# Expert down weights loaded with rows 128 apart in a partition, and the hidden rows turned by two full transpositions

## The reference, cut to what matters

```python
D_MODEL = 1024
N_EXPERTS = N_GROUPS * EXPERTS_PER_GROUP      # 32
D_EXPERT = D_MODEL // 2                       # 512
...
    def expert_block(args):
        xblk, e = args
        return (jax.nn.silu(xblk @ w1[e]) * (xblk @ w3[e])) @ w2[e]
```

## Time and profile before

| | |
|---|---|
| median of 3 runs | 1860.23 us (1854.81 to 1861.74) |
| the profiled execution | 1857.37 us |
| its span in the profile | 1855.5 us, mean granted clock 0.978 |
| TensorE matmul busy | 1718.4 us (93%) |
| VectorE, ScalarE busy | 714.4 us (38%), 594.6 us (32%) |
| moved by DMA | 341.91 MB in 79581 packets, mean 184 GB/s |

### The profile page before, as it was taken

How to read it: one execution, slowest core, us unless ns; L and a number is a source line. 1 busy time by engine, 2 the same in 40 slices (tenths; PEclk the granted TensorE clock), 3 DMA queues, 4 the chain that set the end, 5 groups by cost and what they waited for, 6 DMA issues and landing times.

```text
span 1855.5 us, 24991 instructions
## 1 busy us (share of the span) xinstructions
PE 1718.4 (93%) x10533; PEld 1317.4 (71%) x10533; DVE 714.4 (38%) x1529; ACT 594.6 (32%) x1048; POOL 169.3 (9%) x128
## 2 busy tenths in 40 slices
PE   6999999997999888888889999998999899999998
PEld 5878766886665555455558966666788798888886
DVE  4355454453111111211136577555734532222223
ACT  3434454422010000000124456554524432222222
POOL 1000110221111111101101000011101000000221
PEclk9999999998999999999999999998999999999999
DMA  6512100348999999999995331013420222223201
GB/s 249 192 46 84 53 23 23 135 190 327 356 405 411 410 407 409 405 410 406 414 354 189 97 112 66 1 46 113 171 92 12 91 103 91 92 89 138 91 23 46
DMA packets 79581, 341.91 MB, mean 184 GB/s; under 512 B 8007, under 2 KB 15815, under 8 KB 66024
## 3 DMA queue, kind: packets, MB, share of 16 engines
q1 hardware_dynamic: 73192, 329.76, 45.7%
q0 software_dynamic: 5120, 8.40, 1.3%
q10 hardware_dynamic: 1152, 2.10, 0.3%
HBM read 329.75 MB, written 18.87 MB: 188 GB/s over the span
## 4 chain that ended last, share of the span: by engine, by line
PE 70%; DMA 19%; DVE 5%; ACT 4%; issue 2%; POOL 0%; SPq 0%; DVEq 0%; POOLq 0%; ACTq 0%
PE ps L553 66%; DMA arenaf<-in_w 14%; DMA arenaf<-in_mem 3%; DMA hf<-in_w_xkv 2%; PE ps L972 1%; PE ps L2874 1%; DMA hd<-xf 1%; PE ps L807 1%; PE ps L2057 1%; DVE arenaf L2956 1%; DVE splitr L618 0%; ACT splitr L629 0%; DVE arenaf L2974 0%; ACT arenaf L961 0%; ACT arenaf L868 0%
## 5 line engine op out<-in xcount | busy, mean ns | idle before, releaser
L553 PE MATMUL ps<-hr,splitr 128*128 128x512 f32 (+1 forms) x2784 | 576.3, 367 | 6.8 <-POOL hr L904 4.3
L553 PEld LDWEIGHTS ps<-hr,splitr 128*128 128x128 f32 x2784 | 474.7, 192 | 87.9 <-issue 5.0
L553 PE MATMUL ps<-splitr,hr 128*128 128x512 f32 (+1 forms) x1488 | 273.7, 343 | 2.2 <-DVE hr L1069 1.4
L553 PEld LDWEIGHTS ps<-splitr,hr 128*128 128x128 f32 x1488 | 234.2, 190 | 35.7 <-issue 2.0
L618 DVE TENSOR_TENSOR splitr<-ring,splitr 128x2048 fp32r<-128x2048 f32 x61 | 142.8, 2343 | 232.9 <-ACT splitr L629 232.8
L629 ACT CAST splitr<-ring 128x2048 fp32r<-128x2048 f32 x61 | 116.1, 1904 | 152.2 <-PE ps L553 142.7
L2089 DVE SCALAR_TENSOR_TENSOR arenaf<-ps,arenaf 128x256 f32<-128x256 f32 x32 | 15.5, 484 | 271.9 <-PE ps L553 244.9
L2125 ACT COPY junk<-ps 64x512 f32<-64x512 f32 x32 | 18.5, 578 | 285.6 <-PE ps L553 285.6
L553 PE MATMUL ps<-arenaf 128*64 128x128 f32 (+7 forms) x784 | 103.1, 342 | 5.5 <-ACT arenaf L979 3.5
L553 PE MATMUL ps<-arenaf,tq 128*64 128x512 f32 x336 | 84.9, 651 | 19.5 <-DMA arenaf<-in_w 19.5
L618 DVE TENSOR_TENSOR splitr<-arenaf,splitr 128x2048 fp32r<-128x2048 f32 x27 | 62.2, 2304 | 104.8 <-ACT splitr L629 104.8
(11 more groups left out here) (397 smaller groups left out, 1959.8 us busy)
## 6 DMA issues: line engine op xcount, KB each, us to landing
ring<-in_w SPq DMA_DIRECT2D x22, 2048.0 KB
arenaf<-in_w SPq DMA_DIRECT2D x22, 2048.0 KB, 43.4
splitf<-in_w SPq DMA_DIRECT2D x21, 2048.0 KB
hf<-in_w SPq DMA_DIRECT2D x20, 2048.0 KB, 43.9
ring<-in_w_in SPq DMA_DIRECT2D x11, 2048.0 KB
otf<-in_w SPq DMA_DIRECT2D x11, 2048.0 KB
ring<-in_w_gate_up SPq DMA_DIRECT2D x7, 2048.0 KB
arenaf<-in_w_in SPq DMA_DIRECT2D x4, 2048.0 KB, 8.5
```

The lines of the kernel that those rows point to most:

```text
L553: return te.matmul(out, lhsT, rhs, start=start, stop=stop)
```

## The change

The w2 loads take the view that dense weights have: partition p gets the rows p, 128 + p, 256 + p and 384 + p, so a load is 512 pieces of 4 KB and no longer 128 pieces of 16 KB. Its bytes and its destination are the same in size. The hidden row is now turned in two blocks of 128 contiguous columns, each one a transposition of all 128 partitions. `pe_down` picks the 64-column groups of HCOL in the order that fits. Nothing is changed in the order of the work, in the waits or in w1 and w3.

```diff
             if b:
-                entry("w2", flat, io["w2"][b - 1].rearrange("(p k) n -> p (k n)", k=4))
-        entry("w2", flat, io["w2"][31].rearrange("(p k) n -> p (k n)", k=4))
+                entry("w2", kview(4, 1024), io["w2"][b - 1].rearrange("(k p) n -> p k n", k=4))
+        entry("w2", kview(4, 1024), io["w2"][31].rearrange("(k p) n -> p k n", k=4))
...
-                for k in range(4):
-                    for half in range(2):
-                        a = CAP * half
-                        it = mm(ps[a:a + CAP, CAP * k:CAP * k + CAP], HROW[a:a + CAP, k:256:4],
-                                ident[a:a + CAP, a:a + CAP], True, True)
+                for j in range(2):
+                    it = te.transpose(ps[:, 128 * j:128 * j + 128], HROW[:, 128 * j:128 * j + 128], ident)
...
-                W = thirds(loaded(e), 4)
+                W = loaded(e)
...
-                        it = mm(ps[CAP * half:CAP * half + CAP, :], HCOL[:, k, :],
+                        it = mm(ps[CAP * half:CAP * half + CAP, :], HCOL[:, k % 2 * 2 + k // 2, :],
```

## The result

| | before | changed |
|---|---|---|
| median | 1857.53 us | 1869.70 us |
| range of the runs | 1854.81 to 1861.74 us | 1867.83 to 1870.37 us |
| ratio, 95% interval | | 1.0050 (1.0032 to 1.0068) |
| profiled execution, span | 1857.37, 1855.5 us | 1868.15, 1866.4 us |
| mean granted clock | 0.978 | 0.970 |

The changed kernel is 0.5% slower: 9.3 us by the ratio, between 5.9 and 12.6 us; the two medians are 12.2 us apart. The prediction's sum gave 1867.2 us, in a range of 1856 to 1884 us. One execution of the kernel before, taken beside e1 to e4, lasted 7512 us and is left out of their ratios.

What follows compares the result with a forecast made beforehand. The prediction took DMA transfers to bound the expert stage: 8.1 us of packet cost less 0.5 us gained at the start is 7.6 us; pe_down had 0.6 us to give, leaving 7.0 us: 1860.2 + 7.0 = 1867.2 us, range 1856 to 1884 us.

Steps and rivals of the forecast that it cites:

- The prediction's sum: Whole program: the last pe_down's 7.0 us delay passes through to the end, median from 1860.2 to 1867.2 us.
- What bounds the stage: Expert stage, 510 to 930 us: a transfer limit; the sum of the bytes sets its end, not one load.
- The turning: Hidden row on TensorE: two transpositions take 0.4 us, 0.77 us shorter each, 25 us in all, nearly all under transfers.
- the beginning: Start of the expert stage, 475 to 485 us: an earlier third load gains 0.5 us, between 0 and 0.8 us.
- The packets: w2 loads in the full queue: 4 KB packets cost 0.27 us a load, 8.1 us for 30 (3.0 to 13.8).
- What is late next: Stage end: last pe_down waits for w2, moving 7.0 us; in_w_xkv lands at 959.4 us, TensorE's next work at 961.2 us.
- the 7.6 of the sum: End of the load queue: 8.1 us of packet cost less 0.5 us at the stage's start, 7.6 us later.
- The end: After the expert stage nothing is changed, so the 7.0 us go through to the program's end.
- That packets cost nothing: Rival, chance 0.20: in the full queue engines overlap packets, 4 KB is long enough; 0 to -3 us, 1857 to 1860 us.
- The full descriptor queue: Rival, chance 0.13: more queue entries stall SyncE's issues and starve engines, DMA share below 0.98; +17 us more, 1884 us.
- TensorE as the bound: Rival, chance 0.07: TensorE binds the stage in more places, so shorter turnings gain 8 to 25 us, 1852 to 1836 us.
- What I had held most likely to go wrong: Packet price in the w2 loads: a 4 KB packet in the full queue costs something else than one alone does.

Runs made afterwards that it cites:

- e1: Kernel before with w2 loaded in 4 KB packets (a partition's four rows in falling order), old turning kept; ratio 1.0045, stage 503.2 us.
- e4: Changed kernel with w2 loaded in 1024 packets of 2 KB; ratio 1.0084 against the kernel before, stage 508.1 us.
- e2: Kernel before with its 16 KB loads but the turning in two full transpositions, up products reading weights with a stride; ratio 1.0001, stage 493.4 us.
- e0: Kernel before again, without an edit, as the scale for scatter; ratio 1.0004, stage 493.1 us.
- e8: Changed kernel (4 KB packets in w2) with at most five loads in flight; ratio 1.0052 against the kernel before, stage 500.6 us.
- e7: Kernel e2 (16 KB packets, two transpositions) with at most five loads in flight; ratio 1.0003 against the kernel before, stage 493.9 us.
- e5: Changed kernel with w1 and w3 also in small packets, 2 KB each; ratio 1.0154 against the kernel before, stage +27.0 us.
- e10: Changed kernel with w1 and w3 also in 4 KB packets, so all expert loads are 4 KB; ratio 1.0050 against the kernel before, stage +9.0 us.
- e11: Kernel before with w1 and w3 in 4 KB packets, w2 in 16 KB and the old turning; ratio 1.0080, stage +14.6 us.

## Why the prediction was right

**What bounds the stage.** Right. The bytes in the queue set its end. TensorE's work was made shorter by 0.7 us an expert (one period went from 12.77 us to 523.11 - 511.07 = 12.04 us) and the stage got longer.

**The turning.** 0.4 us was forecast; 0.44 us stands in the rows. As forecast the gain is hidden. The 0.5 us that I had taken for the beginning can't be seen: e2 is at 493.4 us and 1.0001. The rows it rested on are scatter too. In the window from 475 to 485 us the changed kernel has 385 GB/s and not 374, but e0, which has no edit, has 391 GB/s, and in 465 to 475 us a share of 1.00 and not 0.68 (its stage began 3.0 us earlier). The changed kernel's row, then e0's two:

```profile
475.00:485.00 10.00, 9.66 (x80) 6.12 (x82) 1.46 (x3) 0.81 (x2) 0.94 (x1) 1.00 1.02 385
```

```profile
465.00:475.00 10.00, 10.00 (x100) 7.01 (x96) 1.18 (x2) 0.84 (x2) 0.94 (x1) 1.00 1.00 381
475.00:485.00 10.00, 10.00 (x82) 5.73 (x80) 1.87 (x3) 0.95 (x2) 1.69 (x2) 1.00 1.00 391
```

**The packets.** The term was 0.27 us a load between 0.10 and 0.46 us, 8.1 us for 30. The stage measured 6.8 us more, which is 0.23 us a load; e8 against e7 measured 6.7 us; e1, where the turning is the old one, 10.1 us. The three mean 7.9 us. The loads of `in_w_down`, which I had taken as the nearest rows, gave a good price in time for the full queue. There is luck in how well it fits. The three rows lay between 1.6 and 7.3 engine-us, and their mean, 4.3, was taken for a load in the queue. There the mean of three loads rose by 2.5 engine-us, so if only the w2 load got dearer it rose by some 7, at the upper bound; the share of q1 rose from 95.9 to 96.8% at the same time and took a part of it back. The fall of the rate in 600 to 900 us alone, 6.29 MB in 16.05 us before and 16.37 us after, would give 0.32 us an expert and 9.6 us in all, more than the stage shows. Both 0.23 and 0.32 us lie in the forecast of 0.1 to 0.45 us an expert.

The sentence from the Trainium skill, page "DMA: Bandwidth & Descriptors", section "Why small descriptors are slow (HBM only)", would have given 2.6 us, an estimate from its 3 cycles a packet, by the same rule some 1 us for 8 KB and 6 us for 2 KB. The runs say +2.2, +6.8 and +15.0 us. Its form, a fixed price for each packet, agrees with these three; its size is two to three times too small here (nearly four by e1), and the measurement decides. For small packets in all three weights, e5 and e10, a fixed price doesn't hold.

**What is late next.** Right, with small shifts. The last `pe_down` had to wait for its w2 (956.54 us, `[1.05 <-DMA splitf<-in_w]`), where before it had waited for ScalarE. Against the start of the stage it moved by (956.54 - 463.98) - (947.18 - 461.14) = 6.5 us, forecast 7.0. The load of `in_w_xkv` landed at 962.07 us, where 955 to 965 us was forecast. Of the 10.2 us that it moved, 2.8 are the later start of the stage; the other 7.4 us answer to the 7.6 of the sum. The product behind it began 1.85 us later, and 3.7 us after `pe_down` had ended, where 2.38 and 3.4 us stood before; which of the two released it is not shown. The granted clock was 0.95 and not 0.97 in 600 to 900 us, but e0 has 0.95 as well, so this isn't put down to the change.

**The end.** The 7.0 us went through: 6.8 us of stage. That the ratio says 9.3 us and not 6.8 is inside its interval, 5.9 to 12.6 us, and the 4.0 us that the two profiled executions differ outside the stage are of the size that untouched code varies by from one profile to the next. The ratios of e8 and e7 are also 9.1 us apart, with 6.7 us of stage, so a small loss outside the stage is not excluded.

**The rivals.** That packets cost nothing: refuted by the dose, +2.2, +6.8, +15.0 us. The full descriptor queue: its sign came (issues of 13 to 16 us), its effect did not. The point from which it decides, a share under 0.98, was never reached, in no kernel here, with 1.01 to 1.04 from e1 to e11. What made the share fall at 934 to 942 us stays unexplained. TensorE as the bound: refuted by e2 and by the changed kernel beside e1. What I had held most likely to go wrong, that a packet in a full queue costs something else than one alone, did not happen in time for one kind of load (in engine-us it did, as said above); it did for all three together, in e5 and e10.

No kernel here is measurably faster than the one before; e2 and e7 are equal to it. If two transpositions are wanted for their own sake, e2 is the way to have them: order the columns where the up products read them, and leave the loads alone.

## What to carry to other kernels

In a stretch whose DMA share is 1.0, a change of layout that saves TensorE instructions has to be priced by what it does to the packets: here the saving was 32 x 0.73 = 23 us of TensorE time and worth nothing that could be measured, and the packets cost 7 us. Take the price of a packet form from a load of the same form elsewhere in the trace, multiply by the loads in the full queue, and follow it to the first work that waits for the last load. That gave the right size here for one load in three; for all loads it would have given too much (e10: 90 x 0.27 = 24 us, and the stage grew by 9.0). To tell a transfer limit from a starved queue, read share and rate together: here the share stayed at 1.01 to 1.02 with a falling rate, the time went into the packets, and the loss was the same with five loads in flight as with nine.

## What was not expected

- **Stalled issues can be free.** SyncE stood in single issues for 13 to 16 us (into `splitf` 2352 ns in the median, 328 ns at 16 KB in e7), and the share stayed at 1.02.
- **Five loads of 2 MB are enough.** With five in flight and not nine, the rate was 408 GB/s (e7) and 399 GB/s (e8), the ratios 1.0003 and 1.0052. This is a limit on loads in flight, not on places: a load that has landed still holds its place until it is used, and a kernel with fewer places was not tried.
- **Packet prices don't add up.** 4 KB in w2 alone cost 6.8 us, in w1 and w3 alone 14.6 us, in all three 9.0 us; 2 KB in w1 and w3 cost 36.0 us beside 16 KB packets and 27.0 us beside 4 KB packets. The engines' time for a load falls short of the sum of the parts by 2.4 and 3.0 engine-us. The cause is open.
- **Strided reads of the weights by the up products** cost TensorE a little: an up group of 32 instructions stands at 3.79 us in e2 and at 3.62 us in e4, whose reads are contiguous. In e2 it was hidden under the transfers (ratio 1.0001).

The last point's rows, of e2 and of e4:

```profile
464.63 3.79 PE L553 MATMUL ps<-arenaf 128*64 128x256 f32 x32
```

```profile
465.05 3.62 PE L553 MATMUL ps<-arenaf 128*64 128x256 f32 x32
```
